# GLA attention diagonals: from q·k matmuls by chunk to column sums of an element product, on one Trainium2 core

## The reference, cut to what matters

```
b   = cumsum(g)                      # per key dim, within a chunk
att = einsum('bhtd,bhsd,bhtsd->bhts', q, k, exp(b_t - b_s))   # s <= t
o   = att @ v + (q * exp(b)) @ S
```

## Time and profile before

| | us |
|---|---|
| median of 3 runs | 1136.6 (1136.12 to 1136.66) |
| the profiled execution | 1136.95 |
| its span in the profile | 1135.2 |
| TensorE busy | 1122.7 (99%) |
| VectorE busy | 550.4 (48%) |
| ScalarE busy | 430.0 (38%) |
| GpSimd busy | 208.1 (18%) |

### The profile page before, as it was taken

One profiled execution on the slowest core, in us unless ns is written; L12 is line 12 of the kernel. 1 busy time (PEld: TensorE's weight loads), 2 busy tenths in 40 slices (PEclk: granted clock), 3 DMA queues, 4 the chain that ended last, 5 costly groups with the idle time before them and its releaser, 6 DMA issues.

```text
span 1135.2 us, 17658 instructions
## 1 busy us (share of the span) xinstructions
PE 1122.7 (99%) x6902; PEld 1091.0 (96%) x6902; DVE 550.4 (48%) x732; ACT 430.0 (38%) x573; POOL 208.1 (18%) x128
## 2 busy tenths in 40 slices
PE   8999999999999999999999999999999999999997
PEld 7999999999999999999999999999999999999886
DVE  6677777795000001664585376448537003434433
ACT  7344455565111111543653553465344211122311
POOL 3631111122121120110112011111201211120000
PEclk9999999999999999999999999999999999999999
DMA  6221111111212122210221031022102103432332
GB/s 219 50 61 52 49 42 42 42 38 38 75 61 91 57 80 63 75 39 20 79 76 37 23 111 39 18 79 74 37 17 81 37 18 116 164 116 85 102 111 74
DMA packets 95638, 76.25 MB, mean 67 GB/s; under 512 B 3944, under 2 KB 88808, under 8 KB 95608
## 3 DMA queue, kind: packets, MB, share of 16 engines
q1 hardware_dynamic: 85356, 61.79, 18.3%
q10 hardware_dynamic: 10252, 14.06, 3.6%
HBM read 62.04 MB, written 13.80 MB: 67 GB/s over the span
## 4 chain that ended last, share of the span: by engine, by line
PE 97%; ACT 1%; issue 1%; POOL 1%; DVE 0%; ACTq 0%; DVEq 0%; POOLq 0%
PE ps L498 28%; PE ps L499 28%; PE ps L500 28%; PE ps L670 2%; PE ps L712 1%; PE ps L704 1%; PE ps L714 1%; PE ps L697 1%; PE ps L634 1%; PE ps L661 1%; PE ps L532 1%; POOL wlo L458 0%; PE ps L525 0%; ACT whi L925 0%; PE ps L729 0%
## 5 line engine op out<-in xcount | busy, mean ns | idle before, releaser
L498 PE MATMUL ps<-xn,whi 128*128 128x364 f32 (+1 forms) x1344 | 448.6, 334 | 0.6 <-POOL wlo L458 0.6
L500 PE MATMUL ps<-xn,wlo 128*128 128x364 f32 (+1 forms) x1344 | 440.5, 328 | 0.0
L499 PE MATMUL ps<-xn,whi 128*128 128x364 f32 (+1 forms) x1344 | 440.3, 328 | 0.0
L458 POOL TENSOR_TENSOR wlo<-raw,whi 128x1024 fp32r<-128x1024 f32 x72 | 187.4, 2602 | 808.3 <-ACT whi L925 808.3
L498 PEld LDWEIGHTS ps<-xn,whi 128*128 128x128 f32 x1344 | 252.8, 188 | 3.1 <-issue 1.9
L499 PEld LDWEIGHTS ps<-xn,whi 128*128 128x128 f32 x1344 | 252.9, 188 | 0.2
L500 PEld LDWEIGHTS ps<-xn,wlo 128*128 128x128 f32 x1344 | 252.5, 188 | 0.0
L925 ACT ACTIVATE whi<-raw 128x1024 fp32r<-128x1024 f32 x72 | 75.7, 1052 | 152.4 <-PE ps L500 87.1
L499 PE MATMUL ps<-act_s,whi 128*128 128x364 f32 (+1 forms) x384 | 125.9, 328 | 0.0
L498 PE MATMUL ps<-act_s,whi 128*128 128x364 f32 (+1 forms) x384 | 125.7, 327 | 0.0
L500 PE MATMUL ps<-act_s,wlo 128*128 128x364 f32 (+1 forms) x384 | 125.7, 327 | 0.0
(11 more groups left out here) (269 smaller groups left out, 1362.4 us busy)
## 6 DMA issues: line engine op xcount, KB each, us to landing
raw<-in_w_in SPq DMA_DIRECT2D x56, 512.0 KB, 3.8
branch_a<-keep ACTq DMA_DIRECT2D x8, 546.0 KB, 2.8
mal<-branch_a SPq DMA_DIRECT2D x8, 544.0 KB, 4.6
xt<-in_x_prompt SPq DMA_DIRECT2D x8, 512.0 KB, 7.1
raw<-in_w_lru_o SPq DMA_DIRECT2D x8, 512.0 KB, 3.6
st<-in_state_gla ACTq DMA_DIRECT2D x4, 1024.0 KB, 5.3
out<-st ACTq DMA_DIRECT2D x4, 1024.0 KB, 4.4
raw<-in_w_gla_o SPq DMA_DIRECT2D x8, 512.0 KB, 5.4
```

The source lines that it names most:

```text
L458: pool.tensor_tensor(wlo[:, c % 2], raw[:, c % 2], whi[:, c % 2].bitcast(F32), ALU.subtract).then_inc(s["lo_ok"], 1)
L498: pe.matmul(dst, wh, mh, start=first, stop=False)
L499: pe.matmul(dst, wh, ml, start=False, stop=False)
L500: return pe.matmul(dst, wl, mh, start=False, stop=last)
```

## The change

The diagonals are no longer formed by k times q matmuls. VectorE multiplies q and k element by element (times 256, into `vT`, which is free at that time), and the sum over the 128 key dims is a matmul with `ones`, whose 1/256 takes the factor out again. The result has a token's sum in every row, so the same copy with the identity as mask picks the diagonal.

- The product (`scalar_tensor_tensor`, 1024 columns, both inputs in SBUF) comes on VectorE behind `distance(2)`, where the two diagonal copies were.
- It is split in two parts. ScalarE copies the f32r high part into a new tile `dgs`, which lies over `st`, behind `level_exp(2)`; it waits for the product (`dg_prod`) and for the store of the last head's `st`. VectorE subtracts it for the low part behind `keep_level(0)` and signals `dg_lo`. ScalarE waits for that before it fills `vT` with the values.
- A diagonal step is two f32r matmuls of 512 columns, high and low part, with `ones` as the stationary operand, instead of four f32 ones of 128.
- TensorE runs both steps in the middle of piece 0 of job 3, behind level 1, instead of in front of piece 1 of job 2, and waits for `dg_lo`. The list of steps is changed to match: g0, g1, g2, L0, L1, dg0, dg1, L2, vt0a, ...
- The two diagonal copies move on VectorE behind `keep_level(1)`.

```diff
@@ -95,8 +95,9 @@
 def head_steps():
 
 
-    steps = [("g0", "act"), ("g1", "act"), ("g2", "act"), ("dg0", "dve"), ("dg1", "dve")]
-    steps += [("L0", "dve"), ("L1", "dve"), ("L2", "dve"), ("vt0a", "act"), ("vt0b", "act"), ("vt0c", "act")]
+    steps = [("g0", "act"), ("g1", "act"), ("g2", "act"), ("L0", "dve"), ("L1", "dve"),
+              ("dg0", "dve"), ("dg1", "dve")]
+    steps += [("L2", "dve"), ("vt0a", "act"), ("vt0b", "act"), ("vt0c", "act")]
     steps += [("L3", "dve"), ("L4", "dve"), ("L5", "dve"), ("L6", "dve")]
     steps += [("vt1a", "act"), ("vt1b", "act"), ("vt1c", "act"), ("smp", "dve")]
     steps += [("kTa", "act"), ("kTb", "act"), ("kTc", "act"), ("att0", "act"), ("att1", "act")]
@@ -216,6 +217,8 @@
         skeys = at("skeys", [P, NSEQ, P], F32R, w[0])
         kt = work("kt", [P, TOK], F32, TILE)
         kT = work("kT", [P, TTILES, P], F32, TTILES * P * 4)
+        dgs = at("dgs", [P, 2, SEQ], F32R, w[0])
+        assert 2 * SEQ == NCHUNK * DV
         st = work("st", [P, NCHUNK, DV], F32, NCHUNK * DV * 4)
         st0 = work("st0", [P, NSEQ, DV], F32, NSEQ * DV * 4)
         dlast = work("dlast", [P, NCHUNK + NSEQ], F32, 64)
@@ -276,7 +279,7 @@
             "dve_passed", "pe_passed", "sp_passed", "act_passed",
 
             "alo_in", "alo_hi", "alo_lo", "alo_mm", "alo_first", "alo_ok", "wa2_in", "wa2_hi", "wa2_lo", "att_zero", "c_full", "c_act", "c_dve",
-            "g_abs", "g_exp", "g_ln", "g_ok", "b_ok", "q_ok", "k_ok", "lev_d", "lev_e", "lev_qk", "vT_ok",
+            "dg_prod", "dg_hi", "dg_lo", "g_abs", "g_exp", "g_ln", "g_ok", "b_ok", "q_ok", "k_ok", "lev_d", "lev_e", "lev_qk", "vT_ok",
             "kt_d", "kt_e", "kt_ok", "qb_e", "qb_ok", "dlast_ok", "st_ok", "ktm_ok", "att_step", "st0_in", "st_out", "st0_out",
             "smp_hi", "smp_lo", "smask_ok", "sel_ok", "o_sq", "sq_sum", "sq_hi", "sq_lo", "n_rstd", "zg_tanh", "zg_silu", "o_norm", "og0_ok", "og1_ok",
 
@@ -656,10 +659,9 @@
 
                 def diagonal(n):
                     def emit(b):
-                        for c in range(4):
-                            cols = slice((4 * n + c) * P, (4 * n + c + 1) * P)
-                            ins = pe.matmul(ps[:, b, c * P:(c + 1) * P], kb[:, cols], qb[:, cols], start=True, stop=True)
-                        return ins
+                        cols = slice(n * 512, (n + 1) * 512)
+                        pe.matmul(ps[:, b, :], ones[:, :], dgs[:, 0, cols], start=True, stop=False)
+                        return pe.matmul(ps[:, b, :], ones[:, :], dgs[:, 1, cols], start=False, stop=True)
                     c_step(f"dg{n}", emit)
 
                 def level(l):
@@ -774,14 +776,16 @@
                 pe.wait_ge(s["q_ok"], h + 1)
                 part(2, bankA, 0)
                 pe.wait_ge(s["k_ok"], h + 1)
-                diagonal(0)
-                diagonal(1)
                 part(2, bankA, 1)
                 level(0)
                 part(2, bankA, 2)
                 level(1)
                 start_job(3)
-                part(3, bankB, 0)
+                part(3, bankB, 0, EARLY)
+                pe.wait_ge(s["dg_lo"], h + 1)
+                diagonal(0)
+                diagonal(1)
+                part(3, bankB, 0, LATE)
                 level(2)
                 pe.wait_ge(s["vT_ok"], 2 * h + 1)
                 transposes("vt0", vT, "a")
@@ -1161,6 +1165,10 @@
                 act.wait_ge(s["st0_out"], 16 * h + ONE)
                 act.dma_start(st0[:, :, :], t["state_gla"][0].rearrange("b h p v -> h p b v")[h]).then_inc(s["st0_in"], 16)
                 level_exp(2)
+                act.wait_ge(s["dg_prod"], h + 1)
+                act.wait_ge(s["st_out"], 16 * h + ONE)
+                act.activation(dgs[:, 0, :], vT[:, 0:SEQ], ACT.Copy).then_inc(s["dg_hi"], 1)
+                act.wait_ge(s["dg_lo"], h + 1)
                 job_at(2)
                 act.activation(p3(vT[:, :]), slot3(bankA), ACT.Copy).then_inc(s["vT_ok"], 1)
                 hi(3 * h, N_GLA + 4)
@@ -1596,9 +1604,8 @@
                 dve.wait_ge(s["k_ok"], h + 1)
                 level_operands(0)
                 distance(2)
+                dve.scalar_tensor_tensor(vT[:, 0:SEQ], qb[:, 0:SEQ], float(DV), kb[:, 0:SEQ], ALU.mult, ALU.mult).then_inc(s["dg_prod"], 1)
                 dve.wait_ge(s["att_zero"], h + 2)
-                keep_diagonal(0)
-                keep_diagonal(1)
                 for l in range(1, len(LEVELS)):
                     level_operands(l)
                     if l + 2 < len(LEVELS):
@@ -1611,6 +1618,12 @@
                                                     v[:, :, n - 1:n].to_broadcast([P, (c1 - c0) // n, n]), v, ALU.subtract)
                         ins.then_inc(s["kt_d"], 1)
                     keep_level(l - 1)
+                    if l == 1:
+                        dve.wait_ge(s["dg_hi"], h + 1)
+                        dve.tensor_tensor(dgs[:, 1, :], vT[:, 0:SEQ], dgs[:, 0, :].bitcast(F32), ALU.subtract).then_inc(s["dg_lo"], 1)
+                    if l == 2:
+                        keep_diagonal(0)
+                        keep_diagonal(1)
                 keep_level(len(LEVELS) - 1)
                 dve.wait_ge(s["kt_e"], h + 1)
                 dve.tensor_tensor(kt[:, 0:NTOK], kt[:, 0:NTOK], kb[:, 0:NTOK], ALU.mult).then_inc(s["kt_ok"], 1)
```

## The result

The changed kernel takes 1140.63 us (median of 7 runs, 1140.12 to 1141.1), the one before 1136.33 (7 runs, 1136.12 to 1137.0). The ratio is 1.0037, 95% interval 1.0027 to 1.0046: slower by 4.3 us, where 3.9 were forecast on top of 1136.6. The profiled execution has a span of 1138.7 us, 3.5 more than before.

A forecast was written before the change was run, and what follows sets the result against it. TensorE's summed slots bound the kernel: a head -0.87 for cheaper diagonals +1.85 wait at diagonal 1 = +0.98, times four +3.9, from the 1136.6 median giving 1140.5 us; range given 1136.0 to 1141.8.

The forecast's parts named there:

- TensorE's slots: Diagonals on TensorE: 1.78 us a head removed, four 512-column matmuls of 0.227 (0.91) added.
- the missing 0.08: Delay of the second matmul behind an f32 group on TensorE, 0.08 us, not paid between f32r matmuls.
- the 0.87: TensorE's gain a head if nothing waited, 0.87 us; 3.5 us over four heads.
- Where the wait comes: TensorE, second head: no wait at diagonal 0; diagonal 1, asked at 583.21, waits for L1's bank, free at 584.93.
- The size of the wait: TensorE at diagonal 1: 1.85 us a head, from VectorE's steps up to keep_level(1)'s end at 584.93, plus restart and weights.
- GpSimd gets in first at the boundary: Behind distance(2), at 573.97: GpSimd's subtraction goes first and VectorE's product waits until 576.24.
- What lay beside other work: High part 2.0 us early, value copy 1.7 later, level 3's operands at 588, asked after 593: no later wait.
- rival 2: No wait at diagonal 1: L1's bank free by 583.1, full 0.87 a head kept, 1133.1 us; chance 0.08.
- The rule of the Trainium skill: VectorE's product behind distance(2): comes second, since GpSimd asked 0.7 us before; without it 1136.1 us.

The follow-up runs named there:

- the late kernel: Changed kernel's product, split and ones-matmuls moved late in the head, both diagonals between levels 5 and 6: 1133.38 us, ratio 0.9972 to the kernel before.
- the moved copy: Changed kernel with keep_level(1) moved forward on VectorE, right behind the low-part subtraction, before level_operands(2) and distance(4): 1138.82 us, ratio 1.0021 to the kernel before.
- the place alone: Changed kernel with the old eight f32 matmuls of k and q at the new place, without product or split: 1136.48 us, ratio 1.0000 to the kernel before.
- the swapped order: Changed kernel with the product in front of distance(2) instead of behind it: 1140.73 us, ratio 1.0037 to the kernel before.

## Why the prediction was right

*TensorE's slots.* 1.78 for the old group (1.81 shown by leaving it out), 0.227 for 512 columns: the four new ones and the missing 0.08 gave 0.82 of the 0.87 in the late kernel. The step held.

*Where the wait comes.* Diagonal 1 behind the bank of level 1, not diagonal 0 behind the low part: shown by the moved copy, which removed it, and by the place alone, which had none.

*The size of the wait.* Shifted by 0.28, the forecast end of keep_level(1) is 585.21, the row has 585.19; the wait is 1.85 in both. The terms under it held as well, two of them in sum only. The subtraction took its 1.14 (580.68 to 581.82), the steps between it and the copy's end 3.37 of 3.39. Behind GpSimd's end, the product took 1.00 to the next start (577.49) instead of 1.10, and level_operands(1) 1.38 instead of 1.25: whichever operation comes first there is through about 0.13 sooner, and that is the product now, while the earlier trace rows had given it to level_operands(1). Together they are 2.38 instead of 2.35. The start behind the bank took 0.05 instead of 0.03, and 0.10 for the weights. That GpSimd gets in first at the boundary was read from one case; the rows of the changed kernel and the swapped order show it again.

*What lay beside other work.* The high part had 2.0 us, the value copy 3.34 of wait that nobody felt, the transposes' bank 0.9: keep_level(2) ends at 590.25, vt0b starts at 591.13. The prediction said that nothing later becomes a wait, and so it is, but it didn't name that last bank. Its rival 2 was priced too simply for that reason: it took the wait at diagonal 1 as all that stands between the change and 1133.1, and the moved copy, which removes just that, gave 1138.8, since 1.2 us of it by the view's count came back at vt0b.

*The rule of the Trainium skill* (SBUF — State Buffer, Who interferes with whom), that whoever issues first has the shared port for the whole instruction: this case's traces agree, with 3.41 for a product of 1024 columns and 2.41 for one of 64 behind GpSimd's request, against 1.22 in front of it.

*The difference left.* 4.3 us measured, 3.9 forecast, 3.9 in the heads. The remaining 0.4 is outside of them, where nothing was changed. From GpSimd's row at 868.48 to the end of the span are 270.2 us, 269.9 before and 269.9 to 270.4 in the other traces. That and the spread of each kernel's runs, about 1 us, are as large as what is left, and no cause is shown for it.

## What to carry to other kernels

A matmul taken off the busiest engine is only worth its slot if the work that replaces it lands where the other engine idles: here the same product, subtraction and copies cost 4.3 us between levels 1 and 2 and gained 3.1 between levels 5 and 6. Before moving a step in a rotation of banks, look up which step two before it must now be emptied, and when the emptying engine reaches that copy; and when one wait is removed, work out the next bank in the order before counting the gain. Copies from PSUM that run beside GpSimd's subtraction were free here, and taking them away there gave nothing.

## What the runs showed of the hardware that was not expected

How long a VectorE operation with two SBUF inputs stands doesn't depend on how little it has to do: 64 columns took 2.41 us behind GpSimd's subtraction of 1024. The first such operation behind GpSimd's end is also through sooner than in a free stream: by the records, 1024 columns took 1.00 to 1.01 us from that end to the next start (the product in the changed kernel, distance(2) with the product in front of it, the subtraction with the request later), where 1.14 is the distance elsewhere. Delaying GpSimd's request by about 4 us, by an edit on ScalarE alone, made the changed kernel 2.6 us faster, close to the 2.8 of its expectation.
